# Order of the masks, the convolution's shares, the weight splits and the query's rotation in a hybrid block kernel

## The chip, the cores and the metric

The kernel runs on one core of a Trainium2 chip. The metric is the device time of one execution in microseconds (us), given as the median of several runs.

## The reference, cut to what matters

A recurrent mixer block with a convolution branch and a convolutional feed-forward part is followed by two attention layers. T is 512 tokens, the model is 1024 wide, and everything is float32. The change touches these parts:

```python
def _wkv7(...):                       # 8 heads of 64, a state S of 64x64 each, over 512 tokens
    sa = einsum("bhvk,bhk->bhv", S, a_t)
    S = S * w_t + sa * b_t + v_t * k_t
    y = einsum("bhvk,bhk->bhv", S, r_t)
...
c = u[..., :512] * sigmoid(u[..., 512:])
c = _causal_dwconv(c, cconv_w, cconv_b)      # 31 taps, 512 channels
c = silu(_layer_norm(c, cln_g, cln_b))
mix = concatenate([rwkv_out, c], -1) @ w_out
...
# layer 0 of the second block: 16 heads, 32 of the 96 query columns are rotated
q_pe = apply_rope(q_pe, cos, sin)            # x1*cos - x2*sin, x2*cos + x1*sin
```

## The kernel before

**Layout.** Activations lie transposed, channels on the 128 partitions and tokens along the row. Weights come as a stream of 1 MB blocks of 16 tiles of 128x128 (`raw`, two buffers). Each block is split in two float32r parts, `w_hi` and `w_lo`; a product is three matmuls (hi·hi, hi·lo, lo·hi). Block n+2 of the stream can be loaded once block n is split (`split_full`), and block n can be split once block n-2 was used (`block_done`). The engines are programmed by hand with semaphores, and each works through its own list in order.

**The stage around the change.** Blocks 0 to 10 project the input. For blocks 2 to 10 ScalarE writes `w_hi` and GpSimd only `w_lo`. Blocks 7 to 10 give the four channel tiles of the convolution's input: ScalarE takes a sigmoid (`glu_s`), VectorE multiplies (`glu(j)`, L1871) and by that frees the two PSUM banks. The first matrices of the next stage need the banks that `glu(3)` frees.

**The convolution.** `cacc[:, j, :]` gathers 31 taps for tile j. `taps(j)` (L1893) does the first 12 taps on VectorE, 12 instructions of 512 elements. The others are shared: ScalarE multiplies by a tap's weight into one of four buffers (`tap(i)`, L1353), GpSimd adds that to `cacc` (L571). `ADDED` lists them. Before the change tiles 0 and 1 have 12 taps from VectorE, and tiles 2 and 3 have one each from ScalarE (L1361), which leaves 98 adds.

**The units.** For the recurrence, the triangular systems of 64 tokens are inverted by doubling. There are four chunks c of two heads e; a unit is (c, e), and both e run side by side, step by step: `PE_STEPS`, `ACT_STEPS` and `DVE_STEPS` are the orders of the three engines, and each step counts a semaphore (`u_pe`, `u_act`, `u_dve`) that others wait for through `pe_at`, `act_at` and `dve_at`. Of a chunk's steps, L, LT, MT, RB, RK are products into PSUM; DI and DIT set `Di`, `DiT` to the identity on ScalarE; LT on ScalarE copies L transposed from PSUM to `Lt`; D0 and DT0 place the first level in `Di` and `DiT` under a mask (VectorE, copy_predicated, L1963); MT, RB, RK on VectorE mask the products (L1960). TensorE's RK waits for VectorE's MT, MV for RB, Y0 for RK, G1 for D0 and for ScalarE's LT. Levels 1 to 5 follow, each a G, P and Q (all at L768).

ScalarE puts taps between its unit steps (L1392 to L1400): 98 taps over the first 76 of the 80 slots that follow steps other than DI and DIT, so that some slots have two and the slots after DI and DIT none.

**The scan.** Eight steps n of 64 tokens (L785). In step 1 TensorE sums `cacc` for the layer norm after all adds are in, and does the first of the `ada_blocks`, products with 1 MB blocks of another weight that SyncE loads in its queue after the stream's blocks up to 14. SyncE loads block n of the stream when `split_full` reaches n-1:

```python
weights(0, STREAM["out"] + N_OUT)      # blocks 0 to 14
for e in range(2):
    sp.wait_ge(u_pe[e], len(PE_STEPS) * CT)
ada_blocks(0, 6)
```

GpSimd splits blocks 11 and 12 (`split`, both parts, 8 instructions each) after the convolution's adds.

**The first attention layer.** Per head, `top(h, t)` finds row maxima of PSUM tiles (L2205, L2207). TensorE's `tops(h, t)` refills the PSUM pair after `top(h, t-1)`. For the head after the next, `rope_query` makes two products (L2182, L2183) and `rope_query_sum` adds them (L2189), after which ScalarE copies the query. VectorE's order is top 2, `rope_query`, top 3, `rope_query_sum`, top 4.

Of the kernel before, what the change touches and what calls it, by code (L numbers as in the profile page):

```python
# [114 lines left out]
def build(nc, x_t, ctx_t, stream, ada_w, vectors, squares, level_masks, scan_mask, ropes, lora_w, gate_w,  # L115
# [143 lines left out]
    ACT_STEPS = ["DI", "DIT", "LT", "MV", "Y0", "G1", "G2", "G3", "G4", "G5", "W", "U"]  # L259
    DVE_STEPS = ["D0", "DT0", "MT", "RB", "RK"] + [s + str(n) for n in range(1, 5) for s in "PQ"] + ["Q5"]  # L260
    u_pe = [sem(f"unit_tensor{e}") for e in range(2)]
# [40 lines left out]
    SHORT = 12  # L302
    TAPS_LEFT = [TAPS - SHORT] * (CT - 2) + [TAPS - 1] * 2
    ADDED = [(TAPS - left, j) for _, j, left in sorted((-left / TAPS_LEFT[j], j, left) for j in range(CT) for left in range(1, TAPS_LEFT[j] + 1))]

# [228 lines left out]
    def _(pool):  # L534
# [25 lines left out]
        for n in range(2, N_IN):  # L560
            pool.wait_ge(high_done, n - 1)
            for i in range(PARTS):
                ins = low(n, half_of(n), i)
            ins.then_inc(split_full, 1)
        last = {}
        for i, (t, j) in enumerate(ADDED):
            pool.wait_ge(tap_full, i + 3)
            if j in last:
                pool.wait_ge(conv_done, last[j] + 1)
            last[j] = i  # L570
            pool.tensor_tensor(cacc[:, j, :], tap_out[i % 4], cacc[:, j, :], ALU.add).then_inc(conv_done, 1)  # L571

        for n in (STREAM["out"], STREAM["out"] + 1):
            split(n, half_of(n), n // 2)
        before = BLK1 + 2
# [679 lines left out]
    def _(act):  # L1255
# [103 lines left out]
        act.wait_ge(glu_s_free, 2 + CT)  # L1359
        for j in (CT - 2, CT - 1):  # L1360
            act.activation(cacc[:, j, :], cpad[:, j, 0:T], ACT.Identity, scale=col("cconv_w", TAPS * j),  # L1361
                           bias=col("cconv_b", j)).then_inc(tap_full, 1)
        ident4 = ident.unsqueeze(1).broadcast_to([P, 4, P])
# [27 lines left out]

        next_tap = slots = 0  # L1392
        for c in range(CT):
            for step in ACT_STEPS:
                for e in range(2):
                    unit(c, e, step)
                    slots += step not in ("DI", "DIT")
                    while next_tap < min(len(ADDED), slots * len(ADDED) // (2 * CT * (len(ACT_STEPS) - 2) - 4)):
                        tap(next_tap)
                        next_tap += 1  # L1400
# [422 lines left out]
    def _(dve):  # L1823
# [125 lines left out]
        for j in range(1, CT):  # L1949
            if j < CT - 1:  # L1950
                taps(j - 1)
            glu(j)
        def unit(c, e, step):
# [20 lines left out]
            elif step == "D0":  # L1974
                dve.wait_ge(u_pe[e], pe_at(c, "L"))
                dve.wait_ge(u_act[e], act_at(c, "DI"))
                placed(Di[e], bank(0), 0)
            elif step == "DT0":
                dve.wait_ge(u_act[e], act_at(c, "LT"))
                placed(DiT[e], bank(1), 6)  # L1980
            else:
# [196 lines left out]
        def rope_query(h):  # L2178
# [4 lines left out]
            dve.tensor_tensor(qf[e][r, 0:T], wide(2)[r, 0:T], rope[r, 0, :], ALU.mult).then_inc(query_turned, 1)  # L2183

        def rope_query_sum(h):
            e = h % 2
            r = rope_rows(e)
            dve.wait_ge(query_turned, h + 1)
# [29 lines left out]
        rope_query(0)  # L2218
        rope_query_sum(0)
        key_lo(0)  # L2220
        query_lo(0)
        rope_query(1)
        rope_query_sum(1)
        for t in range(5):
# [8 lines left out]
        for h in range(A_HEADS):  # L2233
# [13 lines left out]
            if nxt < A_HEADS:  # L2247
                top(nxt, 3)
            if after < A_HEADS:
                rope_query_sum(after)  # L2250
            if nxt < A_HEADS:
                top(nxt, 4)
# [344 lines left out]
```

## Time and profile before

| | |
|---|---|
| runs | 1980.92, 1987.42, 1989.16 us, median 1987.42 |
| profiled execution | 1980.92 us, span 1979.1 us |
| TensorE matmul busy | 1804.1 us (91%) |
| VectorE, ScalarE, GpSimd busy | 1034.6, 750.9, 950.6 us |
| input projections end, units start | 186.1, 187.8 us |
| units end, scan starts | 378.8, 379.4 us |
| heads of the first attention layer | about 1110 to 1380 us |

Times in a row are from the start of the span. A busy share says how long an engine had work, and not that it set the pace; what an engine waited for stands in brackets behind its row.

### The profile page before, as it was taken

What the parts mean: (1) busy time and instruction counts of PE and PEld (TensorE: products, weight loads), DVE (VectorE), ACT (ScalarE), POOL (GpSimd) and SP (SyncE); (2) the same over time, 40 slices, a digit from 0 to 9 for tenths busy, and PEclk for the clock granted to TensorE, in tenths of its full rate; (3) what the DMA queues carried; (4) which work ended last, traced back from release to release, by engine and by line L of the source; (5) the groups of instructions that cost most, each with busy time, mean ns of one, the idle gap of its engine ahead of it and who ended that gap; (6) DMA issues with size and microseconds to landing.
All of it is one profiled execution on the core that took longest, in us unless ns stands there. A gap on an engine that the chain in (4) does not pass through costs nothing.

```text
span 1979.1 us, 24098 instructions
## 1 busy us (share of the span) xinstructions
PE 1804.1 (91%) x9352; PEld 1417.4 (72%) x9352; DVE 1034.6 (52%) x1221; ACT 750.9 (38%) x1220; POOL 950.6 (48%) x756
## 2 busy tenths in 40 slices
PE   4999899988989999899898999999979999999676
PEld 2778888854748888778587677776847888878554
DVE  4597433326375555300634666666555555666544
ACT  3453555312233333200322455555144344443422
POOL 4453666700639999788354321224624444444122
PEclk8999999999999999999998999999989999999978
DMA  4121000034222222322311100000131111111101
GB/s 171 65 86 43 1 1 1 22 149 167 88 86 86 104 92 99 127 99 93 138 43 64 43 5 18 22 22 22 67 136 43 43 44 43 43 43 43 43 0 43
DMA packets 18572, 126.15 MB, mean 64 GB/s; under 512 B 2064, under 2 KB 2064, under 8 KB 4016
## 3 DMA queue, kind: packets, MB, share of 16 engines
q1 hardware_dynamic: 17760, 119.62, 16.6%
q10 hardware_dynamic: 720, 5.24, 0.7%
q8 instruction: 65, 1.06, 0.2%
q14 instruction: 27, 0.22, 0.0%
HBM read 122.76 MB, written 2.10 MB: 63 GB/s over the span
## 4 chain that ended last, share of the span: by engine, by line
issue 37%; PE 34%; POOL 17%; DVE 5%; ACT 4%; DMA 2%; POOLq 0%; SPq 0%; ACTq 0%; DVEq 0%
POOL w_hi L547 11%; POOL w_lo L539 5%; PE banks L1034 4%; PE banks L768 3%; PE banks L1013 3%; PE banks L628 2%; PE banks L630 2%; PE banks L629 2%; PE banks L641 2%; PE banks L895 1%; PE banks L896 1%; PE banks L900 1%; POOL cacc L571 1%; DMA raw<-in_stream 1%; PE banks L983 1%
## 5 line engine op out<-in xcount | busy, mean ns | idle before, releaser
L547 POOL TENSOR_TENSOR w_hi<-raw,der 128x512 fp32r<-128x512 f32 x300 | 344.8, 1160 | 643.2 <-PE banks L1157 245.1
L539 POOL TENSOR_TENSOR w_lo<-raw,w_hi 128x512 fp32r<-128x512 f32 x336 | 469.5, 1410 | 68.1 <-ACT w_hi L1280 68.1
L628 PE MATMUL banks<-h_hi,w_hi 128*128 128x512 f32 x592 | 235.6, 398 | 18.9 <-DVE h_lo L1845 12.6
L629 PE MATMUL banks<-h_lo,w_hi 128*128 128x512 f32 x592 | 231.5, 391 | 0.0
L630 PE MATMUL banks<-h_hi,w_lo 128*128 128x512 f32 x592 | 231.5, 391 | 0.0
L1154 PE MATMUL banks<-h_hi,w_hi 128*128 128x512 f32 (+1 forms) x384 | 147.8, 385 | 2.8 <-DVE h_lo L2306 2.2
L628 PEld LDWEIGHTS banks<-h_hi,w_hi 128*128 128x128 f32 x592 | 111.6, 189 | 51.8 <-issue 13.7
L1155 PE MATMUL banks<-h_lo,w_hi 128*128 128x512 f32 (+1 forms) x384 | 132.1, 359 | 0.0
L630 PEld LDWEIGHTS banks<-h_hi,w_lo 128*128 128x128 f32 x592 | 111.7, 189 | 23.5
L629 PEld LDWEIGHTS banks<-h_lo,w_hi 128*128 128x128 f32 x592 | 111.8, 189 | 22.8 <-issue 1.0
L1757 ACT ACTIVATE dP<-banks,der 128x768 f32<-128x768 f32 x64 | 57.7, 902 | 170.6 <-DVE der L2341 170.6
L1157 PE MATMUL banks<-h_hi,w_lo 128*128 128x512 f32 (+1 forms) x384 | 117.4, 360 | 0.0
L895 PE MATMUL banks<-h_hi,w_hi 128*128 128x512 f32 (+1 forms) x256 | 93.8, 366 | 13.1 <-POOL w_lo L539 7.4
L588 POOL TENSOR_TENSOR Of<-Of,Ls 128x768 f32<-128x768 f32 x8 | 14.7, 1833 | 186.7 <-DVE Ls L2216 186.7
L2341 DVE TENSOR_REDUCE der<-banks 128x1 f32<-128x768 f32 x64 | 61.0, 953 | 80.9 <-PE banks L1190 80.9
L641 PE MATMUL banks<-ada_raw,sq_c 128*32 128x256 f32 x384 | 90.1, 392 | 13.7 <-DMA ada_raw<-in_ada_w 13.7
L1034 PE MATMUL banks<-Pf,V 128*128 128x512 f32 x192 | 99.0, 597 | 0.3 <-issue 0.3
L2205 DVE TENSOR_REDUCE nmr<-banks 128x1 fp32r<-128x768 f32 x64 | 60.5, 945 | 59.6 <-PE banks L984 58.9
L1595 ACT ACTIVATE Pf<-banks 128x512 f32<-128x512 f32 x112 | 66.6, 595 | 62.7 <-PE banks L1013 60.9
L571 POOL TENSOR_TENSOR cacc<-glu_s,cacc 128x512 f32<-128x512 f32 x50 | 62.8, 1271 | 54.7 <-ACT glu_s L1357 54.5
L1154 PEld LDWEIGHTS banks<-h_hi,w_hi 128*128 128x128 f32 x384 | 73.0, 190 | 22.2 <-DVE h_lo L2306 4.5
L896 PE MATMUL banks<-h_lo,w_hi 128*128 128x512 f32 (+1 forms) x256 | 87.4, 358 | 0.0
(415 smaller groups left out, 4085.0 us busy)
## 6 DMA issues: line engine op xcount, KB each, us to landing
raw<-in_stream SPq DMA_DIRECT2D x84, 1024.0 KB, 4.8
ada_raw<-in_ada_w SPq DMA_DIRECT2D x24, 1024.0 KB, 4.9
xT<-in_x_t SPq DMA_DIRECT2D x2, 1024.0 KB, 6.0
xT<-in_x_t ACTq DMA_DIRECT2D x1, 2048.0 KB, 7.6
out_t<-z SPq DMA_DIRECT2D x8, 256.0 KB, 2.1
ctxT<-in_ctx_t ACTq DMA_DIRECT2D x1, 1024.0 KB, 4.8
rope<-in_ropes ACTq DMA_DIRECT2D x2, 512.0 KB, 3.6
ctx<-in_ctx_t ACTq DMA_DIRECT2D x1, 1024.0 KB, 4.8
```

What stands on the lines that cost most here:

```text
L539: return pool.tensor_tensor(w_lo[:, half, part(i), :], raw_tiles(half)[:, part(i), :], w_hi[:, half, part(i), :], ALU.subtract)
L547: pool.tensor_tensor(w_hi[:, half, part(i), :], raw_tiles(half)[:, part(i), :], one, ALU.mult).then_inc(hi_done, 1)
L628: pe.matmul(banks[b][:, :], hi, rhs_hi[:, k, :], start=(at_k == 0), stop=False)
L629: pe.matmul(banks[b][:, :], hi, rhs_lo[:, k, :], start=False, stop=False)
L630: mm = pe.matmul(banks[b][:, :], lo, rhs_hi[:, k, :], start=False, stop=(at_k == KT - 1))
L641: mm = pe.matmul(banks[ADA_BANK[g]][0:32, 256 * a:256 * a + 256], silu_pad[:, k, :], ada_raws[ADA_RING[g]][:, a, k, :], start=(k == 0), st ...
L895: pe.matmul(out, hi, cols(rhs_hi, k0 + k, a, b), start=(k == 0), stop=False)
L896: pe.matmul(out, hi, cols(rhs_lo, k0 + k, a, b), start=False, stop=False)
L1034: mm = pe.matmul(pairs[1][:, 0, :], v[:, j, :], Pf[:, i % 4, :], start=(j == 0), stop=(j == 5), skip_group_check=True)
L1154: pe.matmul(out, hi, h2_hi[:, k, a:b], start=(k == 0), stop=False)
L1155: pe.matmul(out, hi, h2_lo[:, k, a:b], start=False, stop=False)
L1157: mm = pe.matmul(out, lo, h2_hi[:, k, a:b], start=False, stop=(k == KT - 1))
```

## The change

It has five parts. (A) VectorE's order in a chunk becomes MT, RB, D0, DT0, RK; D0 waits for ScalarE's LT, and DT0 reads `Lt` in SBUF and no longer the PSUM bank. (B) Tile 2 of the convolution gets its first 12 taps from VectorE too, before `glu(3)`; 87 adds are left. (C) GpSimd splits blocks 11 and 12 before the adds. (D) ScalarE does one tap after each unit step, DI and DIT included, until the 87 are done. (E) `rope_query_sum` is part of `rope_query`, so that the sum comes before top 3.

```diff
-    DVE_STEPS = ["D0", "DT0", "MT", "RB", "RK"] + [...]
+    DVE_STEPS = ["MT", "RB", "D0", "DT0", "RK"] + [...]
-    TAPS_LEFT = [TAPS - SHORT] * (CT - 2) + [TAPS - 1] * 2
+    TAPS_LEFT = [TAPS - SHORT] * (CT - 1) + [TAPS - 1]
 # GpSimd
+        for n in (STREAM["out"], STREAM["out"] + 1):
+            split(n, half_of(n), n // 2)
+
         last = {}
         for i, (t, j) in enumerate(ADDED):
-            pool.wait_ge(tap_full, i + 3)
+            pool.wait_ge(tap_full, i + 2)
...
-        for n in (STREAM["out"], STREAM["out"] + 1):
-            split(n, half_of(n), n // 2)
 # ScalarE
-        for j in (CT - 2, CT - 1):
-            act.activation(cacc[:, j, :], cpad[:, j, 0:T], ACT.Identity, scale=col("cconv_w", TAPS * j),
-                           bias=col("cconv_b", j)).then_inc(tap_full, 1)
+        act.activation(cacc[:, CT - 1, :], cpad[:, CT - 1, 0:T], ACT.Identity, scale=col("cconv_w", TAPS * (CT - 1)),
+                       bias=col("cconv_b", CT - 1)).then_inc(tap_full, 1)
...
                     unit(c, e, step)
-                    slots += step not in ("DI", "DIT")
-                    while next_tap < min(len(ADDED), slots * len(ADDED) // (2 * CT * (len(ACT_STEPS) - 2) - 4)):
+                    if next_tap < len(ADDED):
                         tap(next_tap)
 # VectorE
         for j in range(1, CT):
-            if j < CT - 1:
-                taps(j - 1)
+            taps(j - 1)
             glu(j)
...
             elif step == "D0":
-                dve.wait_ge(u_pe[e], pe_at(c, "L"))
-                dve.wait_ge(u_act[e], act_at(c, "DI"))
+                dve.wait_ge(u_act[e], act_at(c, "LT"))
                 placed(Di[e], bank(0), 0)
             elif step == "DT0":
-                dve.wait_ge(u_act[e], act_at(c, "LT"))
-                placed(DiT[e], bank(1), 6)
+                placed(DiT[e], Lt[e][:, :, :], 6)
...
             dve.tensor_tensor(qf[e][r, 0:T], wide(2)[r, 0:T], rope[r, 0, :], ALU.mult).then_inc(query_turned, 1)
-
-        def rope_query_sum(h):
-            e = h % 2
-            r = rope_rows(e)
             dve.wait_ge(query_turned, h + 1)
             dve.tensor_tensor(qf[e][r, 0:T], qf[e][r, 0:T], otmp[r, :], ALU.add).then_inc(query_roped, 1)
```

## Rows read from the trace of the kernel before

**Rows 1.** The page's busy time: share of the span and instructions.

```profile
PE 1804.1 (91%) x9352; PEld 1417.4 (72%) x9352; DVE 1034.6 (52%) x1221; ACT 750.9 (38%) x1220; POOL 950.6 (48%) x756
```

**Rows 2.** The DMA queue's own waits, 140 to 520 us (total, times, longest).

```profile
SPq L499 <- POOL w_lo L539: 255.5, 4, 220.5
```

**Rows 3.** TensorE's timeline from 391 us (start, us, instruction, idle before).

```profile
402.28 5.86 PE L641 MATMUL banks<-ada_raw,sq_c 128*32 128x256 f32 x16 [7.61 <-DMA ada_raw<-in_ada_w]
...
413.66 3.64 PE L641 MATMUL banks<-ada_raw,sq_c 128*32 128x256 f32 x16
```

**Rows 4.** What TensorE waited for, 187 to 380 us.

```profile
PE banks L768 <- ACT Gt L1390: 6.2, 8, 1.2
```

**Rows 5.** VectorE's timeline, 156 to 188 us.

```profile
156.56 12.26 DVE L1896 SCALAR_TENSOR_TENSOR cacc<-cpad,prm,cacc 128x512 f32<-128x512 f32 x11
...
170.47 8.62 DVE L1896 SCALAR_TENSOR_TENSOR cacc<-cpad,prm,cacc 128x512 f32<-128x512 f32 x11
...
186.81 0.69 DVE L1874 TENSOR_TENSOR cpad<-banks,glu_s 128x512 f32<-128x512 f32 x1 [6.99 <-ACT glu_s L1301]
```

**Rows 6.** GpSimd's timeline: four w_lo, and parts of the splits after 377 us.

```profile
158.26 6.86 POOL L539 TENSOR_TENSOR w_lo<-raw,w_hi 128x512 fp32r<-128x512 f32 x4 [3.21 <-ACT w_hi L1280]
...
377.06 2.04 POOL L547 TENSOR_TENSOR w_hi<-raw,der 128x512 fp32r<-128x512 f32 x2
...
383.50 2.49 POOL L539 TENSOR_TENSOR w_lo<-raw,w_hi 128x512 fp32r<-128x512 f32 x2
```

**Rows 7.** GpSimd's timeline in the feed-forward stage.

```profile
711.25 1.49 POOL L547 TENSOR_TENSOR w_hi<-raw,der 128x512 fp32r<-128x512 f32 x1
```

**Rows 8.** VectorE's timeline in the same stretch.

```profile
712.77 1.77 DVE L2110 TENSOR_TENSOR act_lo<-yg,act_hi 128x512 f32 x1 [0.93 <-ACT act_hi L1477]
```

**Rows 9.** VectorE's masked copies, 250 to 650 us (busy, mean ns, idle before).

```profile
L1963 DVE COPY_PREDICATED DiT<-lvl,banks 128x512 f32<-128x512 uint8 x34 | 25.0, 735 | 13.4 <-PE banks L768 10.4 <-ACT Lt L1390 1.9
```

**Rows 10.** TensorE's timeline in chunks 0, 1 and 3 of the units.

```profile
187.76 1.89 PE L773 MATMUL banks<-aB,eA 64*128 64x128 f32 x13 [1.62 <-DVEq L1875]
...
202.88 1.16 PE L768 MATMUL banks<-Gt,DiT 128*128 128x128 f32 x8 [1.17 <-ACT Gt L1390]
...
232.62 1.38 PE L773 MATMUL banks<-aB,eA 64*128 64x128 f32 x13
...
240.63 3.09 PE L773 MATMUL banks<-eR,Q 64*128 64x128 f32 x16 [2.84 <-DVE Gt L1960]
...
247.26 2.79 PE L733 MATMUL banks<-RKt,V_tok 128*64 128x128 f32 x16
...
253.12 2.26 PE L768 MATMUL banks<-Gt,DiT 128*128 128x128 f32 x16 [1.08 <-ACT Gt L1390]
...
330.36 1.37 PE L773 MATMUL banks<-aB,eA 64*128 64x128 f32 x13
...
349.65 2.25 PE L768 MATMUL banks<-Gt,DiT 128*128 128x128 f32 x16
```

**Rows 11.** Windows of chunk 1: busy time per engine, granted clock, DMA share, GB/s.

```profile
246.00:248.00 2.00, 2.00 (x11) 1.88 (x11) 0.00 (x0) 1.28 (x4) 1.26 (x1) 0.50 0.00 0
```

**Rows 12.** ScalarE's timeline, from W of chunk 0 to LT of chunk 1.

```profile
229.90 0.59 ACT L1390 ACTIVATE eA<-banks 64x512 f32<-64x512 f32 x1 [1.65 <-PE banks L739]
230.39 0.71 ACT L1357 ACTIVATE glu_s<-cpad,prm 128x512 f32<-128x512 f32 x1
...
238.65 0.59 ACT L1390 ACTIVATE Lt<-banks 128x512 f32<-128x512 f32 x1
```

**Rows 13.** VectorE's timeline in two heads of the first attention layer.

```profile
1220.98 0.96 DVE L2205 TENSOR_REDUCE nmr<-banks 128x1 fp32r<-128x768 f32 x1 [0.50 <-PE banks L984]
...
1237.43 0.96 DVE L2205 TENSOR_REDUCE nmr<-banks 128x1 fp32r<-128x768 f32 x1
1238.42 1.11 DVE L2189 TENSOR_TENSOR qf<-qf,otmp 32x512 f32<-32x512 f32 x1
```

**Rows 14.** TensorE's timeline in the second of these heads.

```profile
1238.76 0.40 PE L987 MATMUL banks<-KHI,QHI 128*128 128x256 f32 x2
```

More of the change, by code:

```diff
@@ L259, in build @@
     ACT_STEPS = ["DI", "DIT", "LT", "MV", "Y0", "G1", "G2", "G3", "G4", "G5", "W", "U"]
-    DVE_STEPS = ["D0", "DT0", "MT", "RB", "RK"] + [s + str(n) for n in range(1, 5) for s in "PQ"] + ["Q5"]
+    DVE_STEPS = ["MT", "RB", "D0", "DT0", "RK"] + [s + str(n) for n in range(1, 5) for s in "PQ"] + ["Q5"]
     u_pe = [sem(f"unit_tensor{e}") for e in range(2)]
@@ L1390, in unit @@
             act.activation(out, src, ACT.Copy).then_inc(u_act[e], 1)
-        next_tap = slots = 0
+        next_tap = 0
         for c in range(CT):
@@ L2218, in _ @@
         rope_query(0)
-        rope_query_sum(0)
         key_lo(0)
@@ L2222, in _ @@
         rope_query(1)
-        rope_query_sum(1)
         for t in range(5):
@@ L2248, in _ @@
                 top(nxt, 3)
-            if after < A_HEADS:
-                rope_query_sum(after)
-            if nxt < A_HEADS:
                 top(nxt, 4)
```

## The prediction, on record before the result

> **What bounds the kernel now.** I read the page's busy times first: TensorE has matmuls under way 91% of the span [rows 1]. That is a mean over stages, and the change lies in two of them, so I read each by what TensorE waited for.
>
> The units, from 187.8 to 379 us, are a chain through all engines. Before a chunk's RK TensorE stood still for 2.84 us until VectorE had masked MT [rows 10], and afterwards its clock was granted at 0.50, the level of 1.2 GHz, down from 2.4 [rows 11]. In the levels it waited eight times for ScalarE's copy of G, 6.2 us together [rows 4]. Three of these come at Q1 (1.17 and 1.08 us are in [rows 10], the third is alike); the other five share the rest, about 0.55 us each, where ScalarE does two taps between the copies of the two heads.
>
> In the scan TensorE stood still for 7.61 us for the first load of `ada_raw`, then ran that block's 16 matmuls in 5.86 us, where the next block takes 3.64 [rows 3]. The load was late because its queue waited up to 220.5 us for GpSimd's w_lo of block 11 [rows 2], behind the adds. In the attention heads TensorE is practically never idle, so a wait put into its list there costs its full length.
>
> **The start of the units (B and C).** Before, VectorE ended `taps(1)` at 170.47 + 8.62 = 179.09, did `glu(2)`, and then idled 6.99 us before `glu(3)` [rows 5]. `taps(2)` now goes in between: one tensor_scalar (0.55) and the eleven instructions (8.62), 9.2 us, plus 0.4 for the link behind `glu(2)`. So 9.6 us go into a hole of 6.99: 2.6 us late. TensorE's first L waits for `glu(3)`, with 1.62 us of idle time already [rows 10]; nothing covers more.
>
> But the splits of blocks 11 and 12 now start as the projections of blocks 9 and 10 end, at about 172 and 186 us, and lie on top of VectorE's taps. What that does, the trace shows with the same instructions: `taps(0)` took 12.26 us beside four w_lo, `taps(1)` 8.62 without [rows 5], so each w_lo cost VectorE 0.91 us; and each w_lo took 6.86 / 4 = 1.71 us, against 2.49 / 2 = 1.25 alone [rows 6]. The two take turns, one instruction each in 1.7 us. A w_hi is 1.02 us alone [rows 6] and 1.49 beside a VectorE instruction with two SBUF inputs [rows 7]; its turn is 1.45 and costs VectorE 1.45 - 0.78 = 0.67. Two splits are 8 w_hi and 8 w_lo: 8 x 0.91 + 8 x 0.67 = 12.6 us. VectorE has work under all of them: nine instructions of `taps(1)`, then twelve of `taps(2)`, against eight turns each. Start: 2.6 + 12.6 = **+15.2 us**. Bounds: +2.6 if nothing is lost, and 2.6 + 18 = +20.6 if GpSimd's whole time alone (8 x 1.02 + 8 x 1.25) is lost.
>
> The Trainium skill, "SBUF — State Buffer", section "Who interferes with whom", says that a VectorE instruction with two SBUF inputs and a GpSimd instruction that reads SBUF exclude each other for a whole instruction. The trace agrees that they collide, but by that rule a turn would be 1.25 + 0.78 = 2.03 us, where the row has 1.71; by the rule the start would be +20.6 us. It speaks against part A too, as DT0 gets a second SBUF input.
>
> **A chunk of units (A and D).** I count from the start of L. RB's issue ended 2.84 us before 240.63, that is at L + 5.2 (232.62) [rows 10]. VectorE masks MT while TensorE does RB, so RK follows without a gap, and the gap of 2.84 us is gone. RK and MV took 247.26 - 240.63 = 6.6 us at half the clock, so 3.3 to 3.5 at full: MV ends at L + 8.7.
>
> Y0 then needs VectorE's RK, which is now last in line. D0 of the second head waits for ScalarE's LT. That started at 238.65 = L + 6.0 with seven taps between it and W; one tap per slot puts nine there, two more at 0.6 us (a tap takes 0.71 us, overlapped by 0.1) [rows 12]. LT ends at L + 7.8, D0 at 8.6, two DT0 of 0.74 [rows 9] at 10.0, RK at 10.7. DT0 now reads `Lt` and the mask, both in SBUF, while GpSimd adds without a pause. No row has such a copy_predicated. The nearest is the VectorE subtraction of 1.77 us beside a split [rows 8]; its shape takes 0.69 us elsewhere, so up to 1.08 us is lost, and nothing at best: 0 to 2.2 us for the pair. I take 1.5, nearer to the row, since the second DT0 surely meets a fresh add. Y0 starts at L + 12.2.
>
> That leaves TensorE a new gap of 3.5 us before Y0, longer than the old one. So I let the clock fall again: Y0 to Q1 takes 253.12 - 247.26 = 5.9 us as at half clock [rows 10], and 0 to 2.2 us more may be lost in the first level; I take 1. L to Q1: 12.2 + 5.9 + 1 = 19.1 us. Before: 20.5 in chunk 1, 19.3 in chunk 3, and 15.1 in chunk 0, which had no gap [rows 10]. Chunk 2 I take as chunk 3. Gains of 1.4, 0.2, 0.2; chunk 0, which starts on a halved clock, loses 4.2. Together **+2.4 us**. Bounds: with neither collision nor further clock loss 16.6 us each, -7.8 together, and 4 less if the clock stays up; with both at their most 21.0, +9.8.
>
> In the levels every slot has one tap, so the five waits of 0.55 go: **-2.7 us**. GpSimd's 87 adds of some 1.25 us (the shape of w_lo [rows 6]) are 109 us in a stage of 190 and start when the splits are over, so they don't hold ScalarE back, and end before the units do. That 11 taps are dropped is worth nothing by itself.
>
> **The scan (C).** With block 12 split at about 199 us, the queue is free, and the first two `ada_raw` loads go out when the units end, some 15 us ahead of their use; that covers the load, which went out at about 395 and was there at 402.28. The wait of 7.61 and the slow clock, 5.86 - 3.64, go [rows 3]: **-9.8 us**. If the loads were late again, all of it would come back.
>
> **The heads (E).** After the change VectorE does the sum before top 3, and TensorE's next refill (L987) waits for top 3. In six of the fourteen heads with a sum, VectorE runs behind (two reciprocals precede): top 3 runs 1237.43 to 1238.39 without idle time, TensorE comes at 1238.76 [rows 13, 14]. The sum takes 1.11 us there [rows 13], top 3 ends at 1239.53, and TensorE waits 0.84 us. In the other eight, top 3 has 0.50 us of idle time ahead [rows 13] and some 0.4 after, which hold a sum of 0.7. So 6 x 0.84 = **+5.0 us**; 2.4 if the sum takes 0.7, at most 6.8. What comes earlier is ScalarE's copy of the query, which nobody waits for.
>
> **The sum.** 15.2 + 2.4 - 2.7 - 9.8 + 5.0 = +10.1 us. Against the profiled execution (1980.92, of which the span is 1979.1) that is 1991.0. The median run, 1987.42, is 6.5 above the profiled one; a median is what will be compared, so I forecast **1997.5 us**. From no change this measurement can tell about 0.5%, 10 us: my forecast stands on that edge.
>
> **The rivals.**
> 1. VectorE loses nothing to GpSimd, at the splits or at DT0. Start +2.6, chunks -7.8: 2.6 - 7.8 - 2.7 - 9.8 + 5.0 = -12.7, so 1974.7, faster. It decides once the splits cost VectorE less than about 2.5 us (10.1 - 12.6 + 2.5 = 0). For it: no row has w_hi beside a tap. Against: 12.26 beside 8.62 [rows 5]. Chance 0.17.
> 2. They exclude each other for whole instructions: start +20.6, DT0 at 2.2 for the pair (19.8 us from L to Q1, +5.0 in all), heads +6.8: +19.9, 2007.3. For it: the 1.77 us [rows 8]. Against: 1.71 per turn, not 2.03 [rows 6]. The rule of the Trainium skill named above ("SBUF — State Buffer") says this. Chance 0.12.
> 3. The heads hide the sum, because top 3 finds slack in VectorE's list: +5.1, 1992.5. Against it: no idle time in six heads [rows 13]. Chance 0.16.
> 4. Part C doesn't do what it says: TensorE meets another late load in the scan, and 9.8 stays: +19.9, 2007.3. Against it: the loads have 15 us. Chance 0.07.
>
> The forecast itself has 0.45, with a range of its own from +3 to +18 (1990 to 2005); 0.03 is left for the rest.
>
> **Range and chances.** From 1979 to 2011: below lies most of rival 1, above the ends of 2 and 4. Faster by over 0.5%: 0.14, most of rival 1. Slower: half of the forecast, rivals 2 and 4, some of 3, 0.46. Within 0.5%: 0.40.
>
> **What the profile after would show.** `glu(3)` at about 202 us and no longer 187, with TensorE idle some 16 us before L; the taps of VectorE at 1.5 to 1.7 us each beside the splits; no wait for MT before RK, but one of some 3.5 us before Y0, on VectorE's RK; DT0 with durations up to 1.8; no wait for ScalarE's G inside the levels; no wait for `ada_raw` in step 1 of the scan; six waits of 0.8 us at L987's place in the heads. Wrong would make it: taps at 0.78 beside the splits, or a chunk whose clock recovers at once.

## The result, and the profile after

| | before | after |
|---|---|---|
| median (lowest to highest, runs) | 1987.09 us (1980.92 to 1989.16, 5) | 1998.73 us (1994.92 to 1999.40, 5) |
| profiled execution, span | 1980.92, 1979.1 us | 2001.88, 2000.1 us |

The ratio is 1.0058, with a 95% interval of 1.0041 to 1.0076: slower by 0.6%, 11.6 us between the medians. The forecast was 1997.5 us. That it came so close is partly luck: the terms for the start, the levels and the scan were right or near, and the errors of the other two, the start of a chunk and the heads, are large and have opposite signs.

The page's busy times after, which answer to [rows 1], show nothing of where the time went:

```profile
PE 1807.6 (90%) x9352; PEld 1414.9 (71%) x9352; DVE 1065.5 (53%) x1233; ACT 746.1 (37%) x1208; POOL 946.7 (47%) x745
```

So I compare the start times of the same TensorE instructions in both traces: the first product of squares behind the last input block (141.3 us before), the first L of the units (187.8), the first sum over `cacc` (391.0, in step 1 of the scan), the first sum over `csq` behind the scan (435.6), the first refill of the attention heads (1093.4), and the first product with the last head's output (1370.4). The differences between neighbours are each stage's own gain or loss ("units" thus reaches to that first sum). One stage needs a word first. From 62 to 75 us the code is the same in both kernels, but the granted clock was not. Windows of that stretch (busy time of PE, PEld, DVE, ACT, POOL, then the granted clock), after:

```profile
66.00:70.00 4.00, 4.00 (x8) 1.12 (x8) 3.97 (x3) 2.60 (x5) 4.00 (x3) 0.60 0.00 0
70.00:75.00 5.00, 5.00 (x11) 1.06 (x7) 4.08 (x4) 1.87 (x3) 1.49 (x2) 0.50 0.46 157
```

and in the profiled execution of before:

```profile
66.00:70.00 4.00, 4.00 (x12) 1.12 (x12) 3.97 (x3) 3.50 (x8) 4.00 (x4) 1.00 0.00 0
70.00:75.00 5.00, 5.00 (x21) 3.20 (x20) 4.90 (x6) 2.32 (x5) 1.23 (x1) 1.00 0.50 184
```

The profiled execution of before kept 2.4 GHz there, that of after ran at 1.2 GHz and was 6.7 us late at the first landmark. Of the twelve experiments' profiles nine have such a delay, of 4.9 to 6.6 us, and three don't, with the same code up to there. It is a matter of the single execution, and I leave it out: "net" below means without it. Its size fits the 6.2 us by which the profiled execution of before stood under its median of 1987.09.

Net, the changed kernel is 14.3 us later at the end of the span: start of the units +15.0, units -8.3, scan -9.9, from the scan to the heads +1.1, heads +18.1, the rest -1.7 (the sum of the rounded stages is 14.3). Forecast were +15.2, -0.3, -9.8, nothing and +5.0, together +10.1.

**The start.** VectorE's timeline after, which answers to [rows 5]:

```profile
163.26 12.26 DVE L1895 SCALAR_TENSOR_TENSOR cacc<-cpad,prm,cacc 128x512 f32<-128x512 f32 x11
...
177.17 14.97 DVE L1895 SCALAR_TENSOR_TENSOR cacc<-cpad,prm,cacc 128x512 f32<-128x512 f32 x11
...
193.21 1.13 DVE L1893 TENSOR_SCALAR cacc<-cpad,prm 128x512 f32<-128x512 f32 x1 [0.34 <-DVE cpad L1873]
194.37 14.12 DVE L1895 SCALAR_TENSOR_TENSOR cacc<-cpad,prm,cacc 128x512 f32<-128x512 f32 x11
208.52 0.69 DVE L1873 TENSOR_TENSOR cpad<-banks,glu_s 128x512 f32<-128x512 f32 x1
```

GpSimd's timeline under it, the splits of blocks 11 and 12:

```profile
182.78 1.49 POOL L547 TENSOR_TENSOR w_hi<-raw,der 128x512 fp32r<-128x512 f32 x1
184.23 1.74 POOL L539 TENSOR_TENSOR w_lo<-raw,w_hi 128x512 fp32r<-128x512 f32 x1
...
198.30 1.70 POOL L539 TENSOR_TENSOR w_lo<-raw,w_hi 128x512 fp32r<-128x512 f32 x1
199.97 1.48 POOL L547 TENSOR_TENSOR w_hi<-raw,der 128x512 fp32r<-128x512 f32 x1
```

The reader is to see the 8.62 us of `taps(1)` as 14.97, and `glu(3)` at 208.5, with no idle time of 6.99 us before it any more. TensorE waited 16.6 us for it.

**The units.** TensorE's waits from 185 to 390 us (what waited, for what, total, times, longest), which answer to [rows 4]:

```profile
PE banks L774 <- DVEq L1875: 16.6, 1, 16.6
PE banks L734 <- DVE RKt L1958: 13.5, 4, 3.6
PE banks L769 <- ACT Gt L1390: 0.3, 1, 0.3
```

The waits for ScalarE's G, 6.2 us in [rows 4], are gone but for 0.3, and so is the wait before RK. In its place stands one before Y0, 3.6 us long in three of the four chunks. TensorE's timeline in chunk 1, which answers to [rows 10]:

```profile
256.17 1.37 PE L774 MATMUL banks<-aB,eA 64*128 64x128 f32 x13
...
267.84 2.61 PE L734 MATMUL banks<-RKt,V_tok 128*64 128x128 f32 x16 [3.60 <-DVE RKt L1958]
270.38 2.61 PE L769 MATMUL banks<-Di,Lt 128*128 128x128 f32 x16
272.82 2.25 PE L769 MATMUL banks<-Gt,DiT 128*128 128x128 f32 x16
```

**The scan.** TensorE's timeline, which answers to [rows 3]:

```profile
404.39 3.70 PE L820 MATMUL banks<-cacc,sq_c 128*128 128x512 f32 x8
408.02 3.64 PE L642 MATMUL banks<-ada_raw,sq_c 128*32 128x256 f32 x16
```

The block follows without a wait and at full clock.

**The heads.** VectorE's timeline in one of the six heads, which answers to [rows 13]:

```profile
1211.51 0.68 DVE L2179 TENSOR_TENSOR qf<-banks,rope 32x512 f32<-32x512 f32 x1
1212.23 2.10 DVE L2181 TENSOR_TENSOR qf<-qf,otmp 32x512 f32<-32x512 f32 x1
1214.36 0.96 DVE L2197 TENSOR_REDUCE nmr<-banks 128x1 fp32r<-128x768 f32 x1
```

and GpSimd's, TensorE's and the windows of the same stretch:

```profile
1211.96 1.82 POOL L591 TENSOR_TENSOR gate_s<-gate_s,Of 128x768 f32<-128x768 f32 x1
```

```profile
1215.37 0.50 PE L988 MATMUL banks<-KHI,QHI 128*128 128x256 f32 x2 [1.66 <-DVE nmr L2197]
```

```profile
1214.00:1216.00 2.00, 0.63 (x6) 0.63 (x6) 1.37 (x3) 1.33 (x2) 0.00 (x0) 1.00 0.00 0
1216.00:1218.00 2.00, 2.00 (x11) 1.04 (x10) 1.56 (x2) 0.00 (x0) 0.00 (x0) 0.77 0.00 0
1218.00:1220.00 2.00, 2.00 (x13) 1.93 (x12) 0.00 (x0) 0.80 (x1) 0.00 (x0) 0.50 0.00 0
1220.00:1222.00 2.00, 2.00 (x14) 1.67 (x13) 0.00 (x0) 1.16 (x3) 0.00 (x0) 0.88 0.00 0
```

The sum takes 2.10 us, where it took 1.11 behind top 3 [rows 13]. GpSimd's product into `gate_s` has started 0.27 us before it; the sum ends 0.55 us after that product. TensorE waits 1.66 us for top 3, and behind the wait the clock is at 0.50 for about 3.4 us (the shares 0.77, 0.50 and 0.88 of three windows of 2 us make 0.92 + 2.00 + 0.48). By estimate half of that is lost, so such a head costs 1.66 + 1.7, some 3.4 us.

Not every one of the six does. The wait is 1.66 us in all of them, but behind two of them, here the third, the clock stays up:

```profile
1252.33 0.51 PE L988 MATMUL banks<-KHI,QHI 128*128 128x256 f32 x2 [1.66 <-DVE nmr L2197]
1252.00:1254.00 2.00, 1.67 (x12) 1.54 (x13) 1.37 (x3) 0.70 (x2) 0.00 (x0) 1.00 0.04 8
1254.00:1256.00 2.00, 2.00 (x18) 1.54 (x16) 0.56 (x1) 0.88 (x2) 0.00 (x0) 1.00 0.00 0
```

The distances between the six long sums tell the same: 37.0 us from one to the next where the clock fell and 35.4 where it didn't, against 33.5 before. That is 3.5 us for a head with the fall and 1.9 for the one without (the other such head is the last). Together: six waits of 1.66 make 10.0, four falls of 1.7 make 6.8, which leaves 1.3 of the 18.1. Why the clock fell behind four of six equal waits, the same four in e_alone and c_undone below, stays open.

### The profile page after: what moved, and what is told of

Its sections match the earlier page's. It is cut to its first block, busy times and chain, and to the rows that moved or that the text cites. A ratio compares the mean times of both kernels' runs of the same rounds, so it can differ in the third digit from the quotient of the medians.

```text
span 2000.1 us, 24069 instructions
## 1 busy us (share of the span) xinstructions
PE 1807.6 (90%) x9352; PEld 1414.9 (71%) x9352; DVE 1065.5 (53%) x1233; ACT 746.1 (37%) x1208; POOL 946.7 (47%) x745
## 3 DMA queue, kind: packets, MB, share of 16 engines
q1 hardware_dynamic: 17760, 119.62, 16.2%
## 4 chain that ended last, share of the span: by engine, by line
issue 36%; PE 32%; POOL 15%; DVE 11%; ACT 3%; DMA 1%; POOLq 0%; SPq 0%; ACTq 0%; DVEq 0%
POOL w_hi L547 10%; PE banks L769 5%; POOL w_lo L539 5%; PE banks L1035 3%; PE banks L1014 3%; PE banks L642 2%; DVE cacc L1895 2%; PE banks L629 2%; PE banks L630 2%; PE banks L631 2%; PE banks L896 1%; PE banks L897 1%; PE banks L901 1%; DVE nmr L2197 1%; DVE Ls L2208 1%
## 5 line engine op out<-in xcount | busy, mean ns | idle before, releaser
L896 PE MATMUL banks<-h_hi,w_hi 128*128 128x512 f32 (+1 forms) x256 | 93.7, 366 | 13.1 <-POOL w_lo L539 7.4
L2050 DVE TENSOR_TENSOR nacc<-nacc,nt 128x512 f32<-128x512 f32 x14 | 17.3, 1238 | 131.2 <-ACT nt L1438 131.2
```

Of the source, the lines that this page charges most:

```text
L896: pe.matmul(out, hi, cols(rhs_hi, k0 + k, a, b), start=(k == 0), stop=False)
```

## The experiments

Twelve kernels ran, each beside the kernel before. The stages of their profiles against the profiled execution of before, in us, read from the same landmarks; "net" is the whole span without the stretch ahead of the first landmark. The ratio is that of the timed runs to those of the kernel before on the same chip, with its interval.

| run | start | units | scan | to heads | heads | rest | net | median, us | ratio |
|---|---|---|---|---|---|---|---|---|---|
| the change | +15.0 | -8.3 | -9.9 | +1.1 | +18.1 | -1.7 | +14.3 | 1998.73 | 1.0058 [1.0041, 1.0076] |
| e_undone | +15.0 | -9.2 | -10.0 | +1.4 | -0.1 | +0.2 | -2.7 | 1983.06 | 0.9978 [0.9965, 0.9990] |
| e_alone | 0.0 | +1.8 | -0.2 | 0.0 | +18.0 | -1.8 | +17.8 | 2004.95 | 1.0087 [1.0072, 1.0102] |
| e_gate_behind | +15.0 | -7.8 | -10.0 | +0.5 | +3.0 | +0.4 | +1.1 | 1987.01 | 0.9994 [0.9980, 1.0008] |
| e_slack_heads | +15.0 | -9.3 | -9.9 | +0.2 | +0.1 | -1.8 | -5.7 | 1983.52 | 0.9991 [0.9976, 1.0006] |
| c_alone | 0.0 | +2.1 | -9.9 | +0.1 | 0.0 | -1.7 | -9.4 | 1976.32 | 0.9952 [0.9933, 0.9970] |
| c_undone | +2.6 | -9.5 | -9.9 | +1.3 | +18.0 | -1.6 | +0.9 | 1985.68 | 1.0002 [0.9986, 1.0019] |
| a_alone | 0.0 | -8.5 | -0.7 | +0.2 | -0.1 | -1.7 | -10.8 | 1976.44 | 0.9954 [0.9937, 0.9972] |
| bd_alone | +2.5 | +2.7 | -9.9 | +1.1 | -0.1 | +0.1 | -3.6 | 1978.26 | 0.9967 [0.9954, 0.9980] |
| a_psum | 0.0 | -15.0 | -0.6 | -0.5 | 0.0 | -0.1 | -16.2 | 1969.57 | 0.9933 [0.9916, 0.9951] |
| best1 | +2.6 | -10.2 | -9.9 | +1.1 | 0.0 | +0.1 | -16.3 | 1969.78 | 0.9919 [0.9899, 0.9939] |
| best2 | 0.0 | -8.5 | -9.9 | +1.5 | 0.0 | +0.1 | -16.8 | 1967.25 | 0.9918 [0.9900, 0.9936] |
| best3 | 0.0 | -15.7 | -9.9 | -0.3 | 0.0 | 0.0 | -25.9 | 1959.96 | 0.9877 [0.9856, 0.9898] |

The last stages vary by up to 1.8 us with no edit in them. So do the units: e_alone has no edit there and c_alone none to the units themselves, and they stand at +1.8 and +2.1, all of it between L and Q1. The profiled execution of before was thus a fortunate one in this stage, which is part of why the profiles say 14.3 us and the medians 11.6. The median of the kernel before was 1986.01 us beside the four kernels e_, 1983.00 beside c_alone, c_undone, a_alone and best1, and 1983.26 beside the rest.

The units have two sections with different causes: the four stretches from L to Q1, which hold the masks, and the rest, the levels behind Q1. From the starts of the same instructions (before 73.9 and 129.3 us):

| run | order of the masks | taps per slot | L to Q1, four chunks | the rest |
|---|---|---|---|---|
| e_alone | old | old | +1.9 | -0.1 |
| c_alone | old | old | +2.1 | -0.1 |
| bd_alone | old | one | +6.3 | -3.7 |
| a_alone | new | old | -8.2 | -0.4 |
| a_psum | new, DT0 from a bank | old | -15.0 | 0.0 |
| c_undone | new | one | -5.8 | -3.8 |
| the change | new | one | -4.4 | -3.9 |

### The heads: four kernels

**e_undone**, the change without its part in the heads:

```diff
             dve.tensor_tensor(qf[e][r, 0:T], wide(2)[r, 0:T], rope[r, 0, :], ALU.mult).then_inc(query_turned, 1)
+
+        def rope_query_sum(h):
...
             if nxt < A_HEADS:
                 top(nxt, 3)
+            if after < A_HEADS:
+                rope_query_sum(after)
+            if nxt < A_HEADS:
                 top(nxt, 4)
```

> The changed kernel with the sum of the query's rotation put back behind the head's fourth reduction; the other parts of the change stay. Theory: in six heads the early sum meets GpSimd's product into gate_s, takes 2.10 us instead of 1.11, keeps the fourth reduction from TensorE for 1.65 us, and the clock granted after that wait stands at half for some 3.5 us (1.7 us lost), so each costs about 3.0 us and the six 18 us. Then this kernel is 16 to 19 us faster than the changed one: about 1981 where the changed one has 1998.7, and about 6 us faster than the kernel before. Rival: the 18 us are of other origin (the ten stages behind the scan share them, or that execution was unlucky); then it gains what the prediction gave the sum, 5 us, and stands near 1994, some 6 us slower than before.

Measured: 1983.06 us, and the heads are back at -0.1. The timed ratios 1.0058 and 0.9978 differ by 0.0080, some 16 us; the profiles say 18.2 for the heads. The rival of 5 us falls.

**e_alone**, the same lines of the change as the only edit of the kernel before.

> The kernel before with that one edit (the sum straight behind its two products). Theory: +16 to +19 us over the kernel before, about 2004; its trace has the six sums at about 2.1 us, six waits of some 1.6 us of the last product of keys on the fourth reduction, and a granted clock of 0.50 for about 3.5 us behind each. Rival (the cost comes only with the other parts of the change): +5 us, about 1992, with waits of 0.84 us.

Measured: +18.0 us in the heads, 2004.95 us. VectorE's timeline of that kernel has the same sum of 2.10 us:

```profile
1214.13 2.10 DVE L2185 TENSOR_TENSOR qf<-qf,otmp 32x512 f32<-32x512 f32 x1
```

So the loss belongs to this edit alone, and the rest of the change neither adds to it nor lessens it.

**e_gate_behind** keeps the early sum and moves GpSimd's product behind it:

```diff
+            if 2 * p + 5 < A_HEADS:
+                pool.wait_ge(query_roped, 2 * p + 6)
             pool.tensor_tensor(gate_s[:, p, :], gate_s[:, p, :], Of[p % 2][:, :], ALU.mult).then_inc(pair_out, 1)
```

> The changed kernel, in which GpSimd's product into gate_s waits until the early sum of its head is done; the order on VectorE stays as in the change. If the collision with that product is what lengthens the sum, the six sums fall from 2.10 to 0.68 to 1.1 us, the waits of 1.65 us to between 0.2 and 0.7 us, and the kernel gains 10 to 18 us on the changed one: about 1981 to 1989. If it is the order alone that costs (reductions later by a sum, whatever GpSimd does), the waits stay above 0.8 us and it gains less than 8 us.

Measured: 3.0 us in the heads in place of 18.1, 1987.01 us. VectorE's and TensorE's timelines in the head that was shown above:

```profile
1208.56 0.68 DVE L2183 TENSOR_TENSOR qf<-qf,otmp 32x512 f32<-32x512 f32 x1
1209.27 0.96 DVE L2199 TENSOR_REDUCE nmr<-banks 128x1 fp32r<-128x768 f32 x1
```

```profile
1210.28 0.50 PE L990 MATMUL banks<-KHI,QHI 128*128 128x256 f32 x2 [0.24 <-DVE nmr L2199]
```

```profile
1210.00:1212.00 2.00, 1.76 (x13) 1.54 (x13) 1.37 (x3) 0.68 (x2) 1.21 (x1) 1.00 0.00 0
1212.00:1214.00 2.00, 2.00 (x18) 1.60 (x17) 0.51 (x1) 0.93 (x2) 0.00 (x0) 1.00 0.00 0
```

The sum is 0.68 us, the wait 0.24, and behind it the clock stays at 1.00 (the last two lines are windows of that stretch). The order of VectorE's instructions is that of the change; what changed is only whom the sum meets. In this kernel the clock stays up behind all six waits. That settles the cause: of 18.1 us, 15 are the collision with what follows from it, and 3.0 the order.

**e_slack_heads** keeps the early sum in every second head only, where GpSimd has no product beside it:

```diff
+                if h % 2 == 0:
+                    rope_query_sum(after)
             if nxt < A_HEADS:
                 top(nxt, 3)
+            if after < A_HEADS and h % 2:
+                rope_query_sum(after)
+            if nxt < A_HEADS:
                 top(nxt, 4)
```

> The changed kernel with the early sum only in the heads in which GpSimd has no product beside it (every second head); in the others it is back behind the fourth reduction. Theory: in these heads TensorE is not waiting for the fourth reduction, so the early sum costs nothing, and this kernel is within 2 us of the one with the whole edit undone, about 1981. Rival: each early sum costs its own 0.69 us wherever it stands, +5 us over the one with the edit undone.

Measured: +0.1 us in the heads. In these heads the early sum is free, as the prediction had it. (The timed ratio, 0.9991, stands 0.0013 above that of e_undone, and the intervals overlap.)

### The start, the units and the scan: four kernels, and a fifth

**c_alone**, the kernel before with the splits of blocks 11 and 12 ahead of the adds:

```diff
+        for n in (STREAM["out"], STREAM["out"] + 1):
+            split(n, half_of(n), n // 2)
+
         last = {}
         for i, (t, j) in enumerate(ADDED):
...
-        for n in (STREAM["out"], STREAM["out"] + 1):
-            split(n, half_of(n), n // 2)
         before = BLK1 + 2
```

> The kernel before with only the two splits of the out blocks moved ahead of GpSimd's adds. The prediction's steps: no wait for the ada block in the scan (-9.8); the split of block 11 meets VectorE's 11 products of taps(1), which grow from 8.6 to some 14.5 us, but that growth ends inside the 6.99 us in which VectorE waits for ScalarE's gate, so the first L is within 1.5 us of its time; the split of block 12 holds GpSimd's first adds, and by them ScalarE's taps and the copies queued behind them, until some 10 us after the first L, which costs 0 to 5 us in the first chunk. Sum -5 to -10: about 1978. Theory for the changed kernel: its late start comes of the splits together with taps(2), and not of either alone. Rival (the splits alone delay the start): first L 8 to 15 us late, total 0 to +5.

Measured: 1976.32 us, start 0.0, units +2.1, scan -9.9. VectorE's timeline:

```profile
176.90 14.97 DVE L1897 SCALAR_TENSOR_TENSOR cacc<-cpad,prm,cacc 128x512 f32<-128x512 f32 x11
191.91 0.69 DVE L1875 TENSOR_TENSOR cpad<-banks,glu_s 128x512 f32<-128x512 f32 x1
193.28 0.69 DVE L1875 TENSOR_TENSOR cpad<-banks,glu_s 128x512 f32<-128x512 f32 x1 [0.68 <-ACT glu_s L1302]
```

`taps(1)` takes the same 14.97 us as in the change, but the growth of 6.35 us lies in the hole before `glu(3)`, of which 0.68 us is left. Early splits alone cost the start nothing, and the +2.1 in the units is what e_alone has there without any edit. The expectation holds.

**c_undone**, the change with the splits back behind the adds (the diff above, reversed).

> The changed kernel with the splits back behind the adds. Prediction's steps: taps(1) and taps(2) take 8.6 to 8.8 us each and the first L is only 2.6 us later than before, 12.6 us earlier than in the changed kernel; the wait for the ada block in the scan is back (+9.9). The heads keep their 18 us. Sum against the changed kernel -2.7, against before +12: about 1997. Rival (taps(2) itself costs its whole 9 us): the first L 9 us late, no gain on the changed kernel but a loss of some 4 us.

Measured: the start is right, +2.6. The gain on the changed kernel is not 2.7 us but 13.4 (net +0.9 against +14.3), because the wait in the scan did not come back. TensorE's timeline there:

```profile
390.53 3.70 PE L819 MATMUL banks<-cacc,sq_c 128*128 128x512 f32 x8
394.16 3.64 PE L641 MATMUL banks<-ada_raw,sq_c 128*32 128x256 f32 x16
```

and the queue's:

```profile
372.30 9.23 SPq L499 DMA_DIRECT2D raw<-in_stream  x2
381.65 96.58 SPq L507 DMA_DIRECT2D ada_raw<-in_ada_w  x11
```

The `ada_raw` loads go out from 381.65 us on, 12.5 ahead of the first use, although GpSimd splits after its adds. My expectation was wrong here, and with it a step of the prediction.

**a_alone**, the kernel before with VectorE's order and the source of DT0:

```diff
-    DVE_STEPS = ["D0", "DT0", "MT", "RB", "RK"] + ...
+    DVE_STEPS = ["MT", "RB", "D0", "DT0", "RK"] + ...
...
             elif step == "D0":
-                dve.wait_ge(u_pe[e], pe_at(c, "L"))
-                dve.wait_ge(u_act[e], act_at(c, "DI"))
+                dve.wait_ge(u_act[e], act_at(c, "LT"))
                 placed(Di[e], bank(0), 0)
             elif step == "DT0":
-                dve.wait_ge(u_act[e], act_at(c, "LT"))
-                placed(DiT[e], bank(1), 6)
+                placed(DiT[e], Lt[e][:, :, :], 6)
```

> The kernel before with only VectorE's order of a unit changed and the first fill of the transposed tile read from ScalarE's copy; ScalarE's taps keep their old pace. It tells whose the gain of the levels is. Theory: the chunk's start (L to Q1) gains by the order of VectorE, some 4 us over four chunks; the gain inside the levels (3.9 us) comes of one tap per slot and is absent: total -2 to -6, about 1982. The prediction's own figure for the order: +2.4. Rival (all of the levels' gain comes of the taps' pace): 0 to +8 in the four starts.

Measured: 1976.44 us, units -8.5. The gain inside the levels is absent, as expected (-0.4); the start of the chunks gained 8.2 us, twice what I expected. That the whole is as much as the change gains in the units (-8.3) is a coincidence: there it is -4.4 and -3.9. The 8.2 lie between L and Y0: in chunks 1 to 3 Y0 starts 11.0 us behind L, before it was 14.6, 13.1 and 13.4. TensorE's waits from 185 to 376 us:

```profile
PE banks L733 <- DVE RKt L1960: 9.3, 4, 2.8
PE banks L768 <- ACT Gt L1390: 3.4, 6, 0.7
PE banks L773 <- DVEq L1875: 1.6, 1, 1.6
```

The waits for G, 6.2 us before [rows 4], are 3.4: the long ones at Q1 are gone, those of the levels are not. The waits for MT before RK, which the same view of before has as

```profile
PE banks L773 <- DVE Gt L1960: 7.3, 3, 2.8
```

are gone, against 9.3 us in four for RK. What the waits sum to says little: it is 14.3 us here and 15.1 before. The clock says more. One window over all four chunks, before, in a_alone and in a_psum (below):

```profile
187.80:379.40 191.60, 177.39 (x1472) 169.22 (x1473) 79.99 (x114) 111.04 (x196) 124.25 (x101) 0.92 0.01 1
187.60:370.90 183.30, 170.00 (x1474) 163.01 (x1475) 84.10 (x114) 110.91 (x196) 126.79 (x101) 0.94 0.01 1
193.10:369.90 176.80, 166.38 (x1474) 159.02 (x1475) 78.71 (x114) 110.77 (x196) 124.27 (x101) 0.97 0.01 1
```

A mean of 0.92 over 191.6 us is 31 us at the lower level, 0.94 over 183.3 is 22, and 0.97 over 176.8 is 11. If half of that time is lost, an estimate, the clock gives back some 4 to 5 of the 8.5 us.

**bd_alone**, the kernel before with `taps(2)` on VectorE and one tap per slot, drawn up when c_undone had shown no wait:

```diff
-    TAPS_LEFT = [TAPS - SHORT] * (CT - 2) + [TAPS - 1] * 2
+    TAPS_LEFT = [TAPS - SHORT] * (CT - 1) + [TAPS - 1]
...
-                    slots += step not in ("DI", "DIT")
-                    while next_tap < min(len(ADDED), slots * len(ADDED) // ...):
+                    if next_tap < len(ADDED):
...
         for j in range(1, CT):
-            if j < CT - 1:
-                taps(j - 1)
+            taps(j - 1)
             glu(j)
```

> The kernel before with taps(2) on VectorE (87 products on ScalarE in place of 98) and one of them in each slot; VectorE's order of a unit, the splits and the heads as before. It tells what takes the ada block's wait away. The run with the splits late had no such wait although they stood behind the adds. Theory: fewer taps, spread over 87 of the 96 slots, end some 13 us before the units do; the splits behind them are done in time, and the early splits are not needed. Then: start +2.6, levels within 2 us of before, no ada wait in the scan -9.9, together -6 to -9 (about 1977). Rival (the gain of the levels was the taps' pace, and the ada wait goes only with shorter levels): levels -4 or better, or the wait still there: -1 to +2.

Measured: start +2.5, scan -9.9 as the theory said. The 87 taps end earlier in the units, the splits with them, and the load is in time. The units came out at +2.7, outside the 2 us of the theory. In the levels the prediction's gain is there, -3.7 for its -2.7; it is the start of the chunks that lost 6.3. TensorE's wait before RK has grown:

```profile
PE banks L773 <- DVE Gt L1957: 13.8, 4, 4.2
```

(waits from 180 to 480 us; it was 7.3 in three before, and 8.9 in four in e_alone and c_alone). With the old order, VectorE's MT stands behind D0 and DT0, which wait for ScalarE, and ScalarE now has taps behind DI and DIT as well. So the pace of the taps gains some 3.7 us in the levels with either order, and costs at the start of the chunks: 4 to 6 us with the old order, 2.4 with the new one (-5.8 in c_undone against -8.2 in a_alone; Y0 starts 11.7 us behind L, not 11.0). What is left of it in the units, -1.0 and at most +2.7, is little beside the 2 us by which they vary without an edit.

### The fill's source, and three versions

**a_psum**, as a_alone, but DT0 reads TensorE's bank, as before the change:

```diff
             elif step == "DT0":
-                placed(DiT[e], Lt[e][:, :, :], 6)
+                placed(DiT[e], bank(1), 6)
```

> The kernel before with VectorE's new order, but the first fill of the transposed tile reads TensorE's bank, as before, in place of ScalarE's copy. In the run with the order alone, the pair of fills from the copy took 1.32 us in chunk 0, where GpSimd was idle, and 3.09 us in the next, beside GpSimd's adds. Theory: from the bank a pair takes 1.3 to 1.5 us in every chunk, and TensorE's wait for the mask behind it (9.3 us, 4 times) is 1.6 us shorter in three chunks: 3 to 6 us faster than the order alone, 12 to 15 under the kernel before. Rival (the mask's wait is hidden or the clock is lost all the same): within 2 us of the order alone.

Measured: units -15.0, 1969.57 us. VectorE's pair of DT0 in chunk 1 with the copy as source (a_alone):

```profile
240.15 3.09 DVE L1963 COPY_PREDICATED DiT<-lvl,Lt 128x512 f32<-128x512 uint8 x2
```

with the bank (a_psum), in the middle of GpSimd's adds:

```profile
244.94 1.34 DVE L1963 COPY_PREDICATED DiT<-lvl,banks 128x512 f32<-128x512 uint8 x2
```

and in chunk 0 of a_alone, where GpSimd was idle:

```profile
196.18 1.32 DVE L1963 COPY_PREDICATED DiT<-lvl,Lt 128x512 f32<-128x512 uint8 x2
```

The source in SBUF costs 1.75 us for this pair, and only beside GpSimd. TensorE's wait before Y0 fell from 9.3 us to 3.8 in four, but the long waits for G at Q1 are back, 6.0 us in nine against 3.4, so that the waits give only 2.9 of the 6.5 us in the units. The rest fits the clock: half of 22 - 11 us at the lower level is some 5 us, by the same estimate.

**best1** was drawn when the first of these were known: the change without early splits and without its part in the heads, and on SP

```diff
-        weights(0, STREAM["out"] + N_OUT)
+        weights(0, STREAM["out"] + 2)
         for e in range(2):
             sp.wait_ge(u_pe[e], len(PE_STEPS) * CT)
         ada_blocks(0, 6)
+        weights(STREAM["out"] + 2, STREAM["out"] + N_OUT)
```

> A version drawn from the runs so far: the changed kernel with the sum back behind the fourth reduction and the splits behind the adds, and instead the first six ada blocks queued on SP ahead of the last two out blocks, so that the ada load doesn't stand behind a block that waits for a split. Theory: +2.6 (taps(2)) -8 (order and taps' pace) -8 to -10 (ada wait gone without early splits) and nothing in the heads: 12 to 16 us under the kernel before, about 1972. Rival (the out blocks 13 and 14 now come late, behind ada blocks that wait for their buffer): a new wait at the out stage gives back 3 to 10 us, about 1980.

**best2**: the kernel before with a_alone's edit and that of SP; all taps as before.

> The kernel before with VectorE's new order of a unit and, on SP, the first six ada blocks queued ahead of the last two out blocks. All taps as before. Theory: levels -8.5 to -9, ada wait gone -9.9, start unchanged: 17 to 19 us under the kernel before, about 1966, some 2 us under the version with taps(2) on VectorE. Rival: the order on SP matters only together with early splits; then about 1976.

**best3**: the kernel before with a_psum's edit and that of SP.

> The last two together: the new order, the first fill of the transposed tile from the bank, and the ada blocks ahead on SP. Theory: the gains add, 21 to 25 us under the kernel before, about 1962. Rival: as the two before it say.

Measured: 1969.78, 1967.25 and 1959.96 us. In best1 the edit of SP is not what takes the wait away (c_undone had lost it without). In best2 it is: a_alone, with the same taps, kept the wait (-0.7), best2 has -9.9. A new wait in the output stage, best1's rival, doesn't show: the +1.1 and +1.5 up to the heads are no more than e_undone and c_undone have there without that edit (+1.4, +1.3). By the medians best1 and best3 came out in their expected ranges, best2 1 us short of its own (16.0 for 17 to 19). best3 beats both kernels, with a ratio of 0.9877 [0.9856, 0.9898] to the one before. It differs from the change in three small things: it reads a bank instead of a copy, it lets the ada blocks go first in a queue, and it leaves the splits, the taps and the heads alone.

## Why the prediction was right or wrong, point by point

**The start, +15.2: right, +15.0.** The hole of 6.99 us took all of `taps(2)` but 2.6 us; c_undone and bd_alone show 2.6 and 2.5. The collision was put at 12.6, from 0.91 us for each w_lo and 0.67 for each w_hi; the change loses 15.0 - 2.6 = 12.4 us, and the instructions last 1.74 and 1.49 us and start 1.69 and 1.45 apart, where 1.7 and 1.45 were taken. What the prediction didn't say is that B and C don't cost apart: each alone finds the hole (0.0 and +2.5), and together they fill it twice. Rival 1 needed taps at 0.78 us beside the splits and falls.

**A chunk of units, +2.4: wrong in its sign, L to Q1 -4.4.** (By the forecast's own numbers it is +2.2: 19.1 against 15.1 is a loss of 4.0 in chunk 0, not 4.2.) In the four chunks L to Q1 took 18.4, 16.7, 16.9 and 17.5 us, where I had 19.1 for each, 6.9 us less in all. The wait before Y0 is there and as long as predicted (3.6 against 3.5). Y0 started at L + 11.7 in chunks 1 to 3 for L + 12.2, because the pair of DT0 took 2.52 to 2.55 us there and not 2.98; in chunk 0 it took 3.10, and Y0 started at L + 12.6. That is 1.2 of the 6.9 us. The step that failed holds the other 5.7: "I let the clock fall again: Y0 to Q1 takes 5.9 us as at half clock, and 0 to 2.2 us more may be lost in the first level; I take 1". From Y0 to Q1 it was 5.8, 5.0, 5.3 and 5.9 us. The clock did fall; in chunk 1 it is at 0.54 and 0.61 in the windows from 268 to 270 and 270 to 272 us. But it is back at 272, before Q1 starts at 272.82, so the extra 1 us wasn't lost. And the 5.9 us of before held a wait of 1.08 us for G in front of Q1 [rows 10], which is gone too.

**The levels, -2.7: right in mechanism, -3.9.** Every kernel with one tap per slot has -3.7 to -3.9 there, whatever VectorE's order, and none without it more than -0.4. The same pace has a price: with the new order it cost 2.4 us at the start of the chunks (c_undone against a_alone), where two more taps stand ahead of LT and Y0 starts at L + 11.7, not 11.0.

**The scan, -9.8: right in size, -9.9, and put down to the wrong part.** The step "with block 12 split at about 199 us, the queue is free" is true, but it wasn't needed: c_undone and bd_alone have the same -9.9 with late splits. Before, the splits began at 377.06 us, as the units ended; with 87 taps over 87 slots in a stage that ends sooner, c_undone's end early enough for loads at 381.65. In the changed kernel part C thus cost 12.4 us at the start and bought nothing in the scan. This I could have read: the prediction itself says that the adds "end before the units do", and stops there.

**The heads, +5.0 with at most 6.8: wrong, +18.1.** Two steps failed. "The sum takes 1.11 us there" moves a duration along with the instruction. Those 1.11 us were measured behind top 3, where the sum met the tail of GpSimd's product into `gate_s`; moved ahead it meets the whole of it and takes 2.10. And the wait was priced by its length only, where in the units I had let the clock fall behind a wait of 2.84 us; here it fell behind four of six waits of 1.66 us. With the collision taken away the cost is 3.0, inside the forecast's bounds (2.4 to 6.8). Rival 3 (the heads hide the sum) holds for every second head, as the forecast itself said, and falls for the six.

**Rival 2**, exclusion for a whole instruction. For the splits it falls: a turn was 1.74 us, not 2.03. For the sum beside GpSimd's product it nearly fits: the product had started 0.27 us before it and ended at 1213.78, and the sum ended at 1214.33, 0.55 us later, where a sum that waited it out whole would need 0.68. The Trainium skill, "SBUF — State Buffer", section "Who interferes with whom", says that a VectorE instruction with two SBUF inputs contends with a GpSimd instruction that reads SBUF, and that one with at most one such input, outside the modes that use both port pairs, does not. The trace agrees on who contends: the sum and DT0 from the copy do (2.10 for 0.68 us, 3.09 for 1.32), DT0 from a bank doesn't (1.34 for the pair); for DT0's pair the prediction had 1.5 us lost between bounds of 0 and 2.2, and against the 1.32 us of a pair beside an idle GpSimd the changed kernel lost 1.2 in three chunks and 1.8 in the first.

**Rival 4** (the ada load late again) falls.

**The sum.** +10.1 forecast, +14.3 net in the profiles, 11.6 us between the medians: the units came 8.0 us better and the heads 13.1 worse, with 1.1 and -1.7 elsewhere that no step had. The total is right, but an engineer who had acted on its terms would have thrown out part A, which gains 8.5 us in the units by itself, and would have expected the scan's 9.8 us back on taking out part C, which cost 12.4 at the start and was not needed.

## What to carry to other kernels

When an instruction moves, don't take its duration along: look up what the other engine does at the new place, above all for an instruction with two SBUF inputs beside GpSimd. Where a change has several parts that may each cure a wait, ask of each whether the wait would be there without it; slack in an engine's list is spent once, and a wait is cured once. And price a wait of TensorE by the granted clock behind it as well: here one of 1.66 us cost 3.5 us where the clock fell and 1.9 where it didn't, and the order that made one of 0.24, never with a fall, cost 0.5. Last, two sums that agree don't name a cause: a_alone and the change both gained some 8.4 us in the units, and only the split into L to Q1 and the rest shows that half of it came from different parts.

## What the runs showed of the hardware

A masked copy on VectorE of 128x512 takes 0.66 us in a pair from SBUF while GpSimd is idle and 1.3 to 1.6 beside its adds (1.32 for two against 2.52 in the change and 3.09 in a_alone), and 0.67 from PSUM beside the same adds. A sum of two 32x512 tiles in SBUF, 0.68 us by itself, took 2.10 beside a GpSimd product of 128x768 that had started 0.27 us before it and itself took no longer than without it (1.82 us; 1.83 in e_gate_behind): the small instruction pays for the large one. Behind a TensorE wait of 1.66 us the granted clock was at its lower level for some 3.4 us in four of the six heads and stayed up in two; behind the six of 0.24 us it stayed at the upper one. And a stretch of code that no edit touched, 62 to 75 us, ran at either level in different executions, worth 4.9 to 6.7 us, with matmuls under way all the time; what decides it stays open.
